# Reordering the six matmul passes of a contraction slice in the MLPs of a two-layer decoder step

## The reference

```python
def sqrelu_mlp(h, w1, w2):
    return jnp.square(jax.nn.relu(h @ w1)) @ w2

def residual_layer(y, mod, n1, n2, mixer, w1, w2):
    h = modulate(rms_norm(y, n1), mod[0], mod[1])
    out, state = mixer(h)
    y = y + (mod[2] * out).astype(y.dtype)
    h = modulate(rms_norm(y, n2), mod[3], mod[4])
    y = y + (mod[5] * sqrelu_mlp(h, w1, w2)).astype(y.dtype)
    return y, state
```

## Time and profile before

| | us |
|---|---|
| median of 3 runs | 2301.24 |
| the three runs | 2301.24, 2315.24, 2301.0 |
| the profiled execution | 2321.68 |
| its span, first to last instruction | 2320.0 |
| TensorE busy with matmuls | 2071.0 (89%) |
| VectorE busy | 920.8 (40%) |
| ScalarE busy | 529.7 (23%) |

### The profile page before, as it was taken

How to read it: one execution, slowest core, us unless ns; L and a number is a source line. 1 busy time by engine, 2 the same in 40 slices (tenths; PEclk the granted TensorE clock), 3 DMA queues, 4 the chain that set the end, 5 groups by cost and what they waited for, 6 DMA issues and landing times.

```text
span 2320.0 us, 29995 instructions
## 1 busy us (share of the span) xinstructions
PE 2071.0 (89%) x12833; PEld 1808.5 (78%) x12833; DVE 920.8 (40%) x1648; ACT 529.7 (23%) x804; POOL 81.5 (4%) x143
## 2 busy tenths in 40 slices
PE   3887999989999588999999668998895969999997
PEld 2655888857788478999999328976674969999996
DVE  3004434144311636454553229223325464545452
ACT  2124122034422322111111254221003231111111
POOL 2000001400020000000000000000000000000000
PEclk9687999779966698999999879995555989999999
DMA  9543223600130221222223571221101112222211
GB/s 313 194 186 143 98 94 116 218 1 1 37 109 19 73 73 55 87 77 90 72 90 117 208 259 56 91 95 39 57 21 57 55 54 74 90 72 90 85 60 41
DMA packets 137191, 218.62 MB, mean 94 GB/s; under 512 B 6823, under 2 KB 89662, under 8 KB 136398
## 3 DMA queue, kind: packets, MB, share of 16 engines
q1 hardware_dynamic: 124782, 173.32, 22.2%
q0 software_dynamic: 12320, 44.05, 5.5%
HBM read 199.66 MB, written 21.76 MB: 95 GB/s over the span
## 4 chain that ended last, share of the span: by engine, by line
PE 85%; DVE 6%; DMA 3%; ACT 2%; issue 2%; SPq 1%; DVEq 0%; ACTq 0%
PE ps L1183 12%; PE ps L1181 12%; PE ps L1180 12%; PE ps L938 4%; PE ps L940 4%; PE ps L939 4%; PE ps L1107 3%; DMA wring<-in_ada_w 3%; PE ps L861 3%; PE ps L1020 2%; PE ps L1006 2%; PE ps L1268 2%; PE ps L1148 2%; PE ps L1282 2%; PE ps L1149 2%
## 5 line engine op out<-in xcount | busy, mean ns | idle before, releaser
L1180 PE MATMUL ps<-arena_r,wring_r 128*128 128x288 f32 x2048 | 570.9, 293 | 35.0 <-DVE hbuf_r L1826 35.0
L1183 PE MATMUL ps<-arena_r,wring_r 128*128 128x288 f32 x2048 | 440.1, 296 | 0.0
L1180 PEld LDWEIGHTS ps<-arena_r,wring_r 128*128 128x128 f32 x2048 | 386.7, 189 | 35.3 <-DVEq L2051 35.3
L1183 PEld LDWEIGHTS ps<-arena_r,wring_r 128*128 128x128 f32 x2048 | 328.9, 189 | 0.0
L1181 PE MATMUL ps<-hbuf_r,wring_r 128*128 128x288 f32 x1024 | 286.8, 296 | 0.0
L1181 PE MATMUL ps<-arena_r,wring_r 128*128 128x288 f32 x1024 | 284.6, 294 | 0.0
L1577 ACT ACTIVATE wring_r<-wring 128x2048 fp32r<-128x2048 f32 x64 | 122.4, 1916 | 681.0 <-DMA wring<-in_mlp_w 681.0
L1181 PEld LDWEIGHTS ps<-hbuf_r,wring_r 128*128 128x128 f32 x1024 | 194.4, 190 | 0.0
L1181 PEld LDWEIGHTS ps<-arena_r,wring_r 128*128 128x128 f32 x1024 | 192.4, 188 | 0.0
L2076 DVE SCALAR_TENSOR_TENSOR xbuf<-ps,mod,xbuf 128x288 f32<-128x288 f32 (+1 forms) x128 | 56.1, 480 | 249.2 <-PE ps L1183 249.2
L2045 DVE TENSOR_TENSOR wring_r<-wring,wring_r 128x2048 fp32r<-128x2048 f32 x64 | 146.3, 2286 | 17.5 <-PE ps L1151 15.6
(11 more groups left out here) (342 smaller groups left out, 3158.4 us busy)
## 6 DMA issues: line engine op xcount, KB each, us to landing
wring<-in_mlp_w SPq DMA_DIRECT2D x64, 1024.0 KB, 5.2
wring<-in_ada_w SPq DMA_DIRECT2D x24, 2048.0 KB, 17.2
wring<-in_even_w_in SPq DMA_DIRECT2D x14, 1024.0 KB, 5.5
wring<-in_gla_w_in SPq DMA_DIRECT2D x12, 1024.0 KB, 5.3
xspill<-xbuf SPq DMA_DIRECT2D x2, 2304.0 KB, 21.0
xbuf<-xspill SPq DMA_DIRECT2D x2, 2304.0 KB, 9.2
arena<-in_cache_cmp_kv POOLq DMA_DIRECT2D x16, 256.0 KB, 9.2
arena<-in_cmp_w POOLq DMA_DIRECT2D x2, 2048.0 KB, 26.8
```

Of the source, the lines that this page charges most:

```text
L1180: pe.matmul(bank, hi, x_hi[:, k, cols], start=k == 0, stop=False)
L1183: mm = pe.matmul(bank, lo, x_hi[:, k, cols], start=False, stop=k == KC - 1)
```

## The change

Within a slice `k`, the six matmuls are written out one by one. The three on bank 0 come first (`hi * x_hi`, `hi * x_lo`, `lo * x_hi`), and then the three on bank 1, there in the order `lo * x_hi`, `hi * x_hi`, `hi * x_lo`. The flag that opens an accumulation moves with the first pass on each bank (on bank 1 it is now on the `lo` pass), and the one that closes it with the last. The semaphore increment is on the last matmul as before. Nothing else changes: neither the number of instructions, nor operands, buffers, waits or any other engine's stream.

```diff
                                 hi, lo = w_hi[:, k, c * P:(c + 1) * P], w_lo[:, k, c * P:(c + 1) * P]
-                                for bank, cols in zip(banks, halves):
-                                    pe.matmul(bank, hi, x_hi[:, k, cols], start=k == 0, stop=False)
-                                    pe.matmul(bank, hi, x_lo[:, k, cols], start=False, stop=False)
-                                for bank, cols in zip(banks, halves):
-                                    mm = pe.matmul(bank, lo, x_hi[:, k, cols], start=False, stop=k == KC - 1)
+                                pe.matmul(banks[0], hi, x_hi[:, k, halves[0]], start=k == 0, stop=False)
+                                pe.matmul(banks[0], hi, x_lo[:, k, halves[0]], start=False, stop=False)
+                                pe.matmul(banks[0], lo, x_hi[:, k, halves[0]], start=False, stop=k == KC - 1)
+                                pe.matmul(banks[1], lo, x_hi[:, k, halves[1]], start=k == 0, stop=False)
+                                pe.matmul(banks[1], hi, x_hi[:, k, halves[1]], start=False, stop=False)
+                                mm = pe.matmul(banks[1], hi, x_lo[:, k, halves[1]], start=False, stop=k == KC - 1)
                             mm.then_inc(up_mm if j < 4 else down_mm, 1)
```

## The result

In the job that timed the two kernels together, the changed kernel's median is 2325.37 us (10 runs, 2318.55 to 2333.37). The kernel before has 2314.82 us over 10 runs (2301.0 to 2320.89), 13.6 us more than the median of the three runs known ahead. The ratio is 1.0064, 95% interval 1.0040 to 1.0089: slower by 9 to 21 us. The forecast was no change at 2301 us, with 2317 us as the upper end.

What follows compares the result with a forecast made beforehand. The prediction took TensorE's start-to-start matmul distance in the two MLPs (131.6 ns, 6144 times) as the bound. Crossings (-6 to +6 us) and the `token_tile` bound (at most +5) were taken as zero: 2301 us, range 2291 to 2317.

Steps and rivals of the forecast that it cites:

- the first part of the sum: MLP bank crossings: 2048 crossing steps become staying ones, worth -6 to +6 us, taken as zero.
- fourth part: Bank 1 in the MLPs: two neighbours now read the same 288 columns of x_hi; taken as zero.
- The bound from `token_tile`: 13.3 ns over the columns there against 11.6 in the MLPs; half the 1.7 ns difference gives at most +5 us.
- carried to the median: 2301: Whole kernel: profiled run of 2321.68 us lies 20.4 us over the known median 2301.24, so the forecast median is 2301 us.
- Weight changes at nothing: MLP slices: three stationary tile changes instead of two, 1024 more in all, hidden under earlier matmuls; zero taken.
- Evictions and cover: MLP bank evictions: one instruction evicts both halves, so nobody gains; 19 us of room before TensorE would wait.
- Rival A: MLPs: the 11.6 ns excess is paid at bank crossings, 17.4 ns each; 36 us faster, 2266 us; chance 5%.
- rival B: Step from lo to hi pass on bank 1: exposed weight load, 57 ns each, 58 us slower, 2359 us; chance 4%.
- the rhythm: Sign in the profile after: 131 to 132 ns per MLP matmul at full clock.
- the length of the MLPs: Sign in the profile after: the two MLPs again 407 us, with 3072 matmuls each.
- Its own threshold for being wrong: Prediction wrong if the MLPs' length changes by more than 10 us each, or their TensorE clock is no longer 1.00.
- 56 us to win: MLP stream is 9.1 ns above the skill's 122.5 ns; avoiding that over 6144 matmuls could give back an estimated 56 us.

Runs made afterwards that it cites:

- banks_before_halves_after: Against the kernel before: token halves read 0 0 0 1 1 1, banks still written 0 0 1 1 0 1 (another output); 133.33 ns per matmul in both MLPs.
- cross_all: Kernel before reordered so all six steps of a slice cross banks (0 1 0 1 0 1), still two weight changes; 133.33 ns per matmul, 2324.13 us.
- after_windows_256: Changed kernel with its second column window starting at 256 instead of 288 (another output); 131.67 ns per matmul in both MLPs, 2324.66 us.
- cross_three_changes: Kernel before reordered to banks 0 1 1 0 0 1, with three weight changes and a repeated read; 131.67 ns per matmul, ratio 0.9995 when timed.
- one_window_aligned: Kernel before with all six passes reading columns 0 to 287 (another output); 131.67 ns per matmul.

## Why the prediction was wrong, point by point

What bounds the kernel held: the MLPs grew only through the start-to-start distance, and TensorE got no new wait.

**The step that failed** is the first part of the sum, where the order of the six neighbours was priced by whether a step stays on a bank or crosses, and set to zero. The term is +10.2 us: 133.33 ns in place of 131.67, in each of 6144 matmuls. Its cause is not the bank (`banks_before_halves_after`), and it is no price per kind of step, staying or crossing (`cross_all`). The steps in the traces repeat, to 1 ns, in a fixed cycle: of two slices where the kernel before is at 131.67 ns, of one where it is at 130.00 and in the changed kernel, and of four matmuls in `cross_all`, in both runs with one window and in `after_windows_256`. Which cycles occurred went with the order in which the two column windows are read, together with where the second one starts. The windows were in the edit beside the banks, yet the prediction named them only in its fourth part, as a repeated read of the same columns. It was right that the repeated read costs nothing (`cross_three_changes`).

The bound from `token_tile` came near in size, by luck as far as the runs show. Its excess over the columns is 13.3 ns, and the changed kernel's is 133.33 - 120 = 13.3 too. The prediction halved the 1.7 ns by counting steps, for +5 us; the whole of it came. But `token_tile` has one window of 512 columns, and neither of the two causes that the bound was meant for (staying, weight changes) is at work in the MLPs.

Reading for a price per step was the wrong tool, and finer starts would not have helped. In the trace behind those rows the four staying steps of two slices average 130.1 ns and the eight crossing ones 132.5. Priced by that, 2048 fewer crossings give back 5 us, where the run lost 10. Each rhythm has its own pattern of steps, and only whole slices can be compared.

**The second miss** is the baseline, the step "carried to the median: 2301". Three runs, two of them at 2301, were taken for the kernel's level, and the profiled 2321.68 us for the outlier. Ten runs put the median at 2314.82, 13.6 us higher. Neither miss alone leaves the range: 2301 + 10.2 = 2311, and a median of 2315 with no change are both under its upper end of 2317. Together they give 2325. The rhythms have a part in that spread: 130.00 against 131.67 is worth 1.67 x 6144 = 10.2 us. The run at 130.00 took 2314.3 us, so they don't explain all of it.

Weight changes at nothing: right, by two, three and four per slice at one rhythm. Evictions and cover: right, no wait of TensorE in the loop. Rival A (a cost per crossing) and rival B (57 ns per exposed weight load) are both refuted; B had the sign but neither the place nor the size.

Of the signs that it named, the rhythm (133.33 instead of 131 to 132 ns) and the length of the MLPs (412 us instead of 407) failed. Its own threshold for being wrong, more than 10 us in each MLP, was too wide to notice: they grew by about 5 us each.

The Trainium skill's N / 2.4 + 2.5 ("TensorE: Matmul & The Clock Gate", Back-to-back issue gap) is given there for an isolated matmul, and the page itself says that it under-counts at small N in a stream of loads and matmuls. The distance of the stream to 122.5 ns was therefore no sign of 56 us to win. No rhythm here came under 130.00 ns.

**What stays open.** What makes the cycle, and why a window from column 288 (1152 bytes after a chunk's start) is slower than those from columns 0 and 256 (0 and 1024 bytes), was not measured; three starts don't give a rule of alignment. Nor is it known what picks 130.00 or 131.67. Where the activation buffers lie as a whole, and which columns of the weight tile a load reads, were not varied between runs. A price per window doesn't fit either: the kernel before reads from column 288 in half of its matmuls and has been at 130.00 ns, below the 131.67 of the stream that reads from column 0 alone. The window runs were executed once each, with two MLPs that agreed, while the window order of before has shown that one order can have several rhythms. Of the 10.6 us between the medians, 10.2 are the MLPs' when both sides are at their usual rhythm; how often before is at 130.00 in plain runs can't be read from total times. No version beat both kernels: the kernel before is at 131.67 or 130.00, and no order or window reached less than 130.00.

## What to carry to other kernels

In a dense stream of matmuls, count how many a fixed stretch holds and compare whole periods of the pattern, since a change of order can shift the rhythm by 1% with no step that stands out at 10 ns. Reordering matmuls that alternate between column windows need not be free where the windows start differently; look at the start address of what is read rather than at the bank written. And one profiled execution shows one rhythm: run the unchanged kernel again before a difference of 1% is put down to the edit.

## What the runs showed of the hardware that was not expected

- The distance between matmul starts, averaged over 192 of them at full clock, took only a few values, each constant through an MLP of 3072 matmuls: 130.00, 131.67 and 133.33 ns (780.0, 790.0 and 800.0 ns per slice of six). Two MLPs of variants were outside these, one at 134.4 and one that went around 134.3. Single steps differ, from 125 to 140 ns in these three rhythms. The columns alone are 288 / 2.4 = 120 ns. At 1.2 GHz it is 240 ns in the kernels before and changed alike.
- A long step can recur without regard to what is computed: every fourth is 140 ns in `cross_all` and 135 ns in `one_window_aligned`, in slices of six.
- The same instructions showed 134.4 ns in one MLP and 130.0 in the other of one execution, and 131.67 in both of the next.
- A stream that reads one window only ran at 131.67 ns from column 0 and at 133.33 from column 288.
- Whether neighbouring matmuls write one PSUM bank or two left no mark: with 0, 2 or 4 staying steps of six, streams ran at 133.33 ns (`cross_all`, `banks_before_halves_after`, the changed kernel).
